# Feed-forward of a two-block transformer layer stack: eight of eleven gate/up units computed with the weight blocks stationary

## The reference

```python
D_MODEL = 1024
D_FF = -(-8 * D_MODEL // (3 * 256)) * 256        # 2816

def _rmsnorm(x, g):
    y = xf * lax.rsqrt(jnp.mean(xf * xf, axis=-1, keepdims=True) + EPS)
    return (y * g.astype(jnp.float32)).astype(x.dtype)
...
h2 = _rmsnorm(x, g_ffn[l])
x = x + (jax.nn.silu(h2 @ w_ffn_gate[l]) * (h2 @ w_ffn_up[l])) @ w_ffn_down[l]
```

## Time and profile before

| | |
|---|---|
| median of 3 runs | 1126.32 us |
| the profiled execution's own time | 1126.38 us |
| its span, first to last instruction | 1124.5 us |
| around the span | 1.9 us |
| PE matmul busy | 1116.1 us (99%), 5384 instructions |
| DVE busy | 694.4 us (62%) |
| ACT busy | 635.6 us (57%) |
| POOL busy | 165.4 us (15%) |
| granted TensorE clock | 1.0 in all 40 slices |
| DMA | 205 MB, 182 GB/s on average |
| units ffn3 to ffn10 on PE | 302.70 to 393.61 us |

### The profile page before, as it was taken

The page is one execution under the profiler, slowest core; times in us unless marked ns, Lnnn a source line. Parts: engine busy times, 40 slices in busy tenths (PEclk is TensorE's granted clock), DMA queues, the critical chain, the costliest instruction groups (busy, mean ns, idle before and its releaser), DMA issues.

```text
span 1124.5 us, 14167 instructions
## 1 busy us (share of the span) xinstructions
PE 1116.1 (99%) x5384; PEld 932.7 (83%) x5384; DVE 694.4 (62%) x731; ACT 635.6 (57%) x791; POOL 165.4 (15%) x115
## 2 busy tenths in 40 slices
PE   9999999999999999999999999999999999999997
PEld 7788888888888888888888888888888888888886
DVE  5745668775655543696548568764465776777442
ACT  6655566654867643654587366563355545666331
POOL 1434700000433310000023011000016100200000
PEclk9999999999999999999999999999999999999999
DMA  9645444555555555665435455555555334455530
GB/s 354 234 168 185 131 168 160 197 187 187 188 189 184 186 188 187 223 235 187 150 112 195 161 194 199 223 189 189 192 186 205 127 132 169 166 208 203 209 113 37
DMA packets 30501, 205.14 MB, mean 182 GB/s; under 512 B 3624, under 2 KB 3792, under 8 KB 6768
## 3 DMA queue, kind: packets, MB, share of 16 engines
q1 hardware_dynamic: 28752, 198.75, 49.0%
q0 software_dynamic: 1696, 5.64, 1.6%
HBM read 203.33 MB, written 1.05 MB: 182 GB/s over the span
## 4 chain that ended last, share of the span: by engine, by line
PE 94%; DVE 3%; ACT 1%; issue 1%; DMA 1%; SPq 0%; DVEq 0%; ACTq 0%
PE ps L690 74%; PE ps L1187 8%; PE ps L1189 4%; PE aux L762 3%; PE ps L812 1%; PE aux L978 1%; PE aux L1138 1%; DMA mrows<-in_mem 1%; ACT Wh L1311 1%; PE aux L1125 0%; PE aux L1076 0%; DVE sc L2473 0%; DVE Wl L1876 0%; PE aux L964 0%; DVE bprob L2488 0%
## 5 line engine op out<-in xcount | busy, mean ns | idle before, releaser
L1876 DVE TENSOR_TENSOR Wl<-raw,Wh 128x2048 fp32r<-128x2048 f32 x184 | 428.6, 2336 | 239.6 <-ACT Wh L1311 239.2
L690 PE MATMUL ps<-Wh,xT 128*128 128x512 f32 x1536 | 485.9, 392 | 0.0
L1311 ACT ACTIVATE Wh<-raw 128x2048 fp32r<-128x2048 f32 x184 | 350.0, 1907 | 239.6 <-PE ps L690 218.3
L690 PEld LDWEIGHTS ps<-Wh,xT 128*128 128x128 f32 x1536 | 288.4, 188 | 59.9 <-issue 0.7
L690 PE MATMUL ps<-Wl,xT 128*128 128x512 f32 x768 | 298.9, 389 | 0.0
L690 PEld LDWEIGHTS ps<-Wl,xT 128*128 128x128 f32 x768 | 144.3, 188 | 29.0
L1187 PE MATMUL ps<-xT,Wh 128*128 128x512 f32 x384 | 133.6, 394 | 0.0
L1189 PE MATMUL ps<-xT,Wl 128*128 128x256 f32 x384 | 106.5, 277 | 0.0
L690 PE MATMUL ps<-Wh,hTh 128*128 128x512 f32 x256 | 99.7, 389 | 0.0
L690 PE MATMUL ps<-Wh,hTl 128*128 128x512 f32 x256 | 99.6, 389 | 0.0
L690 PE MATMUL ps<-Wl,hTh 128*128 128x512 f32 x256 | 99.6, 389 | 0.0
(11 more groups left out here) (362 smaller groups left out, 1297.0 us busy)
## 6 DMA issues: line engine op xcount, KB each, us to landing
raw<-in_wstream SPq DMA_DIRECT2D x185, 1024.0 KB, 4.8
grow<-in_post_gains POOLq DMA_DIRECT2D x4, 512.0 KB, 5.5
grow<-in_b_gate POOLq DMA_DIRECT2D x6, 256.0 KB, 3.5
mrows<-in_mem SPq DMA_DIRECT2D x2, 512.0 KB, 5.4
raw<-in_wstream SPq DMA_DIRECT2D x2, 512.0 KB, 6.6
x<-in_x SPq DMA_DIRECT2D x1, 1024.0 KB, 13.6
out<-x SPq DMA_DIRECT2D x4, 256.0 KB, 2.0
rdm<-in_ret_decays POOLq DMA_DIRECT2D x1, 768.0 KB, 5.0
```

The source lines that it names most:

```text
L690: mm = nc.tensor.matmul(ps[2 * pair + t][:, :], a[:, kt, t * P:(t + 1) * P], w[:, slot, j, :], start=(first and j == 0 and q == 0), stop=( ...
L1311: nc.scalar.activation(Wh[:, slot, 0:nk, :], raw[:, slot, 0:nk, :], ACT.Copy).then_inc(hi_ready, 1)
L1876: nc.vector.tensor_tensor(Wl[:, slot, 0:nk, :], raw[:, slot, 0:nk, :], Wh[:, slot, 0:nk, :].bitcast(F32), ALU.subtract).then_inc(lo_ready, 1)
```

## The change

Units 0 to 2 stay as they are (`FF_ROWS = 3`). Units 3 to 10 (`FF_COLS`) are computed as the `up` units are, with the weight blocks stationary. A row's norm factor can then no longer be applied by ACT when it reads PSUM, because tokens lie along the free axis. So the turned x is multiplied with it beforehand: DVE adds high and low part of `xT` to `xs`, makes two diagonal matrices `dg` of the factors, PE multiplies them with a matrix of ones (`x1r`: the factors spread over all partitions), DVE multiplies `xs` by it, and ACT and DVE split it anew in `xn`. For each unit ACT copies the low half of each PSUM bank to `fpart`, DVE adds the high half into `guc`, and POOL, ACT and DVE go on as before; the transposes of units 3 to 10 and their reads from PSUM go.

```diff
+            def swiglu_columns(n, i):
+                pool.wait_ge(sem("lsig_ready"), count + 2)
+                pool.wait_ge(sem("ff_read"), i * 8 + 4 * (n - FF_ROWS + 1))
+                gup = guc[:, n % 2, 0:2, :]
+                nc.gpsimd.tensor_tensor(gup, gup, guc[:, n % 2, 2:4, :], ALU.mult).then_inc(sem("ff_prod"), 1)
...
+                nc.gpsimd.tensor_tensor(gup, gup, fe[:, n % 2, :, :], ALU.mult).then_inc(sem("ff_h"), 1)
...
+            def spread_x1():
+                pe.wait_ge(sem("x1_diag"), 1)
+                o = open_aux("x1r")
+                for t in range(2):
+                    mm = nc.tensor.matmul(o[:, t * P:(t + 1) * P], K("ones"), dg[:, t, :], start=True, stop=True)
...
+            def ff_columns(n, i):
+                for c in range(4):
+                    if isinstance(i, int) and n == FF_ROWS:
+                        wait_drained(pe, f"ffn{n - 2 + c // 2}", c % 2)
+                    else:
+                        pe.wait_ge(sem("ff_read"), i * 8 + (4 * (n - FF_ROWS) + c - 3))
...
-            begin(["ffn0", "ffn1"], "x1T", x, added("wout1"))
+            begin(["ffn0", "ffn1"], "x1T", x, added("wout1"), {(1, 2): spread_x1})
             ff_unit(2, None, lambda: ff_turned(0))
             ff_turned(1)
-            with pe.Fori(1, 5) as i:
-                for n in (1, 2):
-                    ff_unit(n, i)
-                    ff_turned(n - 1, i)
+            pe.wait_ge(sem("xn_low"), 2)
+            ff_columns(3, 0)
+            ff_turned(2)
+            ff_columns(4, 0)
+            with pe.Fori(1, 4) as i:
+                ff_columns(3, i)
+                ff_columns(4, i)
...
+            def ff_columns(n, i, late=None):
+                low_part(n, i, 0)
+                low_part(n, i, 1)
+                act.wait_ge(sem("ff_h"), count - 1)
+                act.wait_ge(sem("ff_read"), i * 8 + (4 * (n - FF_ROWS) + 2))
+                nc.scalar.activation(e, guc[:, n % 2, 0:2, :], ACT.Abs).then_inc(sem("ff_abs"), 2)
...
+                nc.scalar.activation(e, e, ACT.Exp, scale=-1.0).then_inc(sem("ff_exp"), 1)
...
+                nc.scalar.activation(e, e, ACT.Ln, bias=1.0).then_inc(sem("log_ready"), 1)
+                low_part(n, i, 2)
+                act.wait_ge(sem("lsig_ready"), count + 2)
+                nc.scalar.activation(e, e, ACT.Exp).then_inc(sem("ff_rec"), 1)
+                low_part(n, i, 3)
+                split(G[name] + RING, i)
+                split(GEND[name] - 1 + RING, i)
...
+                act.wait_ge(sem("ff_h"), count + 1)
...
+                nc.scalar.activation(dst[:, count, :, :], guc[:, n % 2, 0:2, :], ACT.Copy).then_inc(sem("ffT_hi"), 1)
...
             ff(0)
+            xn_high()
             ff(1)
...
+            nc.vector.tensor_tensor(xs[:, :, :], f32(xTh), f32(xTl), ALU.add).then_inc(sem("xn_sum"), 1)
             x_stats("x1")
...
                 split(G[name] + RING, i)
+                if n == 0:
+                    xn_rows()
                 log_sigmoid(fe[:, n % 2, :, :], gu[:, n % 2, :, 0:256], n + 2 if i is None else i * 2 + (n + 2))
...
+            def ff_columns(n, i, before=None, late=None):
+                add_part(n, i, 0)
+                add_part(n, i, 1)
+                if before:
+                    before()
+                log_sigmoid(fe[:, n % 2, :, :], guc[:, n % 2, 0:2, :], i * 2 + (n + 2))
+                add_part(n, i, 2)
+                add_part(n, i, 3)
+                split(G[name] + RING, i)
+                split(GEND[name] - 1 + RING, i)
...
             ff(0)
+            xn_low()
             ff(1)
```

More of the change, by code:

```diff
@@ L96 @@
 RET_V = [f"ret{n}" for n in range(4, 8)]
+FF_ROWS = 3
+FF_COLS = [f"ffn{n}" for n in range(FF_ROWS, FFN // 256)]
 def plan_drain():
@@ L168, in plan_aux @@
     use("x1T", [0, 1, 2, 3])
-    for n in range(FFN // 256):
+    use("x1r", [3])
+    for n in range(FF_ROWS):
         use(f"ffT{n}", [n % 2])
@@ L357, in build @@
         fe = at("fe", [P, 2, 2, 256], R + 52)
+        guc = at("guc", [P, 2, 4, TOK], R + 44)
+        xn = at("xn", [P, 2, DK, TOK], R + 56, F32R)
+        xs = at("xs", [P, DK, TOK], R + 64)
+        fpart = at("fpart", [P, 4, TOK], R + 72)
+        dg = at("dg", [P, 2, P], R + 72)
         RQ = at("RQ", [P, 2, D], R)
@@ L1078, in ff_turned @@
                 tr.then_inc(aux_ready[k], 1)
-            begin(["ffn0", "ffn1"], "x1T", x, added("wout1"))
+            def spread_x1():
[3 more added lines that the diff above has]
+                    mm = nc.tensor.matmul(o[:, t * P:(t + 1) * P], K("ones"), dg[:, t, :], start=True, stop=True)
+                done(mm, "x1r")
+            def ff_columns(n, i):
+                name = f"ffn{n}"
+                for c in range(4):
[3 more added lines that the diff above has]
+                        pe.wait_ge(sem("ff_read"), i * 8 + (4 * (n - FF_ROWS) + c - 3))
+                    o = ff_bank(c)
+                    w = slice(c * P, (c + 1) * P)
+                    for kt in range(DK):
+                        g = G[name] + kt // 4
+                        if c == 0 and kt % 4 == 0:
+                            pe.wait_ge(lo_ready, i * 4 + (g + 1))
+                        nc.tensor.matmul(o[:, :], Wh[:, g % RING, kt % 4, w], xn[:, :, kt, :], start=(kt == 0), stop=False,
+                                         skip_group_check=True)
+                        mm = nc.tensor.matmul(o[:, 0:TOK], Wl[:, g % RING, kt % 4, w], xn[:, 0, kt, :], start=False,
+                                              stop=(kt == DK - 1), skip_group_check=True)
+                        if c == 3 and kt % 4 == 3:
+                            mm.then_inc(gran_used, 1)
+                        elif kt == DK - 1:
+                            mm.then_inc(half_done if c == 1 else sem("ff_done"), 1)
@@ L1088, in ff_ready @@
             def ff_ready(q):
                 def go_on():
-                    if q == 3:
-                        ff_turned(10)
                     for n in range(2 * q, min(2 * q + 2, FFN // 256)):
-                        wait_operand(f"ffT{n}", (0,))
-                return go_on
-            product("ffd0", (ffTh, ffTl), before={q: ff_ready(q) for q in range(6)})
-            product("ffd1", (ffTh, ffTl), leave=RING)
+                        if n < FF_ROWS:
+                            wait_operand(f"ffT{n}", (0,))
+                        else:
+                            pe.wait_ge(sem("ff_low"), n - FF_ROWS + 1)
@@ L1098, in _, with ff_free @@
+                return go_on
+            def ff_free(c0):
+                return lambda t: pe.wait_ge(sem("ff_read"), 4 * len(FF_COLS) - 4 + c0 + t + 1)
+            product("ffd0", (ffTh, ffTl), before={q: ff_ready(q) for q in range(6)}, bank_free=ff_free(0))
+            product("ffd1", (ffTh, ffTl), leave=RING, bank_free=ff_free(2))
             tile_by_tile(steps_of(["ffd1"], (ffTh, ffTl)), {(1, 1): next_tile("x2T", x, added("ffd1"), 0)})
@@ L1615, in _ @@
             ff_high(1)
[L1616 to L1619, removed]
+            ff_columns(3, 0, lambda: ff_high(2))
+            ff_columns(4, 0)
+            with act.Fori(1, 4) as i:
+                ff_columns(3, i)
+                ff_columns(4, i)
             for g in range(G["ffd0"], GEND["ffd0"]):
                 split(g + RING)
-                if g == G["ffd0"] + 2:
-                    ff_high(10)
             for g in range(G["ffd1"], GEND["ffd1"] - RING):
@@ L2230, in _ @@
             ff_low(1)
[L2231 to L2234, removed]
+            ff_columns(3, 0, None, lambda: ff_low(2))
+            ff_columns(4, 0, lambda: columns_low(3, 0))
+            with dve.Fori(1, 4) as i:
+                ff_columns(3, i, lambda: columns_low(2, i))
+                ff_columns(4, i, lambda: columns_low(3, i))
             for g in range(G["ffd0"], GEND["ffd0"] - 1):
                 split(g + RING)
-                if g == G["ffd0"] + 2:
-                    ff_low(10)
+                if g == G["ffd0"]:
+                    columns_low(4, 3)
             add_rows("ffd0", 0)()
```

80 lines of the change are left out of this document (74 added, 6 removed).

## The result

The changed kernel took **1132.8 us** (median of 6 runs, 1131.75 to 1133.03) against 1126.3 before (6 runs, 1126.22 to 1126.63): ratio 1.0055, 95% interval 1.0045 to 1.0064. That is 6.5 us slower, inside the range and 1.6 over the forecast. The profiled execution took 1133.03 us with a span of 1131.2, 6.7 more than before.

The account below looks back on a forecast made before the run. The prediction took the kernel as bound by PE, busy 99% of the span. Its terms, -2.2 + 0.5 + 3.8 + 2.8 = +4.9 us on 1126.38, gave 1131.2 us, with a range of 1127.4 to 1134.4.

Parts of the forecast that it names:

- PE's own work: Units 3 to 10 on PE: eight transpose groups go, 256 pairs at 0.3467 us replace 384 matmuls, -2.2 us.
- The moving operand in two pieces: Pairs of units 3 to 10, high and low 8 KB apart: no extra taken, at most under 0.1 us a matmul.
- Spread factors: Two fp32 matmuls of 128 columns on PE's path, with change of form and back: +0.5 us.
- Start-up wait: Ahead of unit 1's transposes PE waits for POOL's hidden rows, pushed back in the DVE and POOL queue: +3.8 us.
- late starts: Units 8, 9, 10 and the down projection start late, waiting for DVE's addition once slack is gone: +2.8 us.
- Cycle 11.9 against 11.09: Later units: serial steps of DVE, ACT and POOL take 11.9 us a unit against PE's 11.09; slack 2.4 us.
- One wait only: Rival, chance 0.20: only the start-up wait with unit cycle under 11.5, or 1 us at the start plus the cycle's 2.8; 1128.5.
- Nothing waits: Rival, chance 0.16: DVE's second split and POOL's hidden rows run side by side, cycle below 11.5, no waits; 1124.7.
- Longer cycle: Rival, chance 0.11: 0.06 us more in each of nine hand-overs, cycle 12.5, late starts sum to 6; 1134.4.
- Cheap pairs: Rival, chance 0.03: matmuls cost N/2.4 + 2.5 ns by the skill's formula, so pairs are cheaper; 1129.8.

Follow-up runs that it names:

- preparation alone: The kernel before plus the preparation of xn (sum, diagonal, spread, multiplications, copies, subtractions), which nobody reads, all units still turned: 1131.92 us, ratio 1.005.
- joined kernel: The changed kernel with high and low part of xn side by side instead of 8 KB apart: 1132.33 us, ratio 1.0052.
- three edits: The changed kernel with unit 1's transposes two blocks later, DVE's next two additions ahead of its second split, and xn's parts side by side: 1126.24 us, ratio 0.9998.
- nudge of 128 columns: The changed kernel with all three edits plus one unread 128-column matmul between the transposes of unit 2 and unit 4: median 1126.35 us, two of 11 at 1124.76 and 1124.97.
- one of 256: The changed kernel with all three edits plus one unread 256-column matmul between the transposes of unit 2 and unit 4: 1126.35 us.
- additions first: The changed kernel with DVE adding the next unit's first two blocks ahead of its second split of this unit: 1131.4 us, ratio 1.0045.

## Why the prediction was right, and where not

- **PE's own work, -2.2: mis-sized.** "Where it is one piece there are the rows above, and I take no extra": the extra was 0.0067 us a pair, but all 256 pairs paid it, 1.7 us. The step that failed is carrying the price of the earlier trace rows over from the second block. There it is steady, 0.3467 in all 14 profiles; in the gate/up units the same form mostly takes the other level. The moving operand in two pieces, which I had named as the risk, doesn't decide it: both layouts have both levels.
- **Spread factors, +0.5: right** within what starts differ by (0.2 between executions).
- **Start-up wait, +3.8: right** in mechanism, engines, order and size (3.55), and the preparation alone makes it.
- **Behind the wait: a term was missing.** I priced the idle time of PE at its length. The gap also let the clock fall in the profiled execution, for another 2.6 us. The terms that were off are +2.6 here, +1.7 for the pairs and -2.3 for the late starts, so that the sum came within 2 us partly by luck: two errors one way and one the other. The last two nearly cancel for a reason, as dearer pairs leave less for the cycle to exceed.
- **Cycle 11.9 against 11.09: the cycle was right (11.81), what hangs on it mis-sized.** (11.9 - 11.09 is 0.81; the sum took 0.85 a unit, which is about 0.25 of the 2.8.) The steps of the forecast (2.8, 3.5, 4.5, 6.4 us from the second split's end) read 2.83, 3.44, 4.36, 6.30 in the rows. The late starts were 0.5, not 2.8, because PE's unit took 11.31 (dearer pairs): from the addition at 329.74 to that at 400.63 there are six cycles, each 0.50 longer than PE's unit, 3.0 in all, and 3.0 - 0.5 leaves a slack of 2.5, forecast 2.4. Where pairs ran mostly at 0.3467, in the joined kernel, the same waits sum to 1.5 (0.53, 0.52 and 0.5, with what each costs the matmul behind it).
- **Rivals.** "One wait only", 1128.5, had the cycle under 11.5, and it is 11.81; its small late starts came all the same, by the dearer pairs. "Nothing waits", 1124.7, was made by hand with three edits and gave 1126.2; the 1.5 between are the pairs (seven units of 32 at 0.0067 more). "Longer cycle" did not come. "Cheap pairs" is out, 0.353.

## What to carry to other kernels

The price of idle time on PE is its length and, in most executions here, a stretch at half clock behind it. On the way to a PE-bound stage look at what one-off preparation pushes back in DVE's and POOL's queue, and give PE the work that is already fed (turning unit 1 two blocks later was worth 5.8 us, almost all of the loss). Where matmuls of two widths alternate, take no pitch of such a pair from another stage. Group them by width where the trace shows the dearer level: 2.794 us a block beats 2.827, but not the 2.773 that the second block's up units already have. A change that saves 0.27 us a unit on PE, as here, is used up by any one of these.

## What was not expected of the hardware

- Around a gap of 3.4 us without matmuls the granted clock fell to 0.50, for 6.8 us in one profiled execution (2.6 us lost) and for 3.4 us in two (1.6 lost in each); in a fourth the same 3.41 us left it at 1.00. The Trainium skill, "TensorE: Matmul & The Clock Gate", section "Loop structure matters more than you think", says that a long wait between matmuls makes PE run cold; the trace agrees in three of these executions and not in the fourth.
- A pair of a 512- and a 256-column matmul has two stable pitches, 0.3467 and 0.3533 us, on the full clock, with the same operands and no wait; it changed only at interruptions. What chooses between them stays open. Shown is that the layout of xn doesn't, that a wait can be followed by either, that the second block's up units have 0.3467 in every profile, and that in the gate/up units grouping by width takes away some of the extra; a nudge of 128 columns was followed by runs 1.5 us faster in two of 11, one of 256 in none of ten. A phase of the matmuls against their weight loads or against another engine would fit, and was not tried.
- DVE's two splits of a unit took 5.59 together where two alone take 4.56 (2.28 each in the rows of additions first), and POOL's hidden rows lie between them: the exclusion read from the earlier trace rows holds in every unit.
